# Seven block products for the queries of a cross attention: 14 units of half a block instead of 8 blocks

## What is computed

```python
q = (hn @ w_xq).reshape(Bsz, S, N_XHEADS, DH_X)      # hn = rmsnorm(h) * gain, S = 1024, D = 1024
kv = mn @ w_xkv                                       # mn: 256 normalised memory tokens
s = jnp.einsum('bshd,bmhd->bhsm', q, k) * (DH_X ** -0.5)
p = jax.nn.softmax(s, axis=-1)
o = jnp.einsum('bhsm,bmhd->bshd', p, v).reshape(Bsz, S, D_MODEL)
h = h + o @ w_xo
```

## Time and profile before

| | us |
|---|---|
| median of 3 runs (2746.62 to 2751.62) | 2748.8 |
| profiled execution, its own time | 2748.8 |
| its span in the trace | 2747.0 |
| keys and values (from 386.8 to 438.8) | 52.0 |
| queries, block 41 to the last but one matmul group (from 438.8 to 523.3) | 84.5 |
| TensorE's granted clock, mean | 0.994 of full speed |

### The profile page before, as it was taken

One profiled execution on the slowest core, in us unless ns is written; L12 is line 12 of the kernel. 1 busy time (PEld: TensorE's weight loads), 2 busy tenths in 40 slices (PEclk: granted clock), 3 DMA queues, 4 the chain that ended last, 5 costly groups with the idle time before them and its releaser, 6 DMA issues.

```text
span 2747.0 us, 35390 instructions
## 1 busy us (share of the span) xinstructions
PE 2690.7 (98%) x12702; PEld 2202.3 (80%) x12702; DVE 1782.2 (65%) x2101; ACT 1122.8 (41%) x1862; POOL 1338.7 (49%) x782
## 2 busy tenths in 40 slices
PE   8999999999999999999999999999999999999999
PEld 6888787878778888888887777778887788888886
DVE  7888643345866666976845456884548655557776
ACT  4256623132433333443413525563457333334444
POOL 4323123455689999100466321555165788884002
PEclk9999999999999999999999999999999999999999
DMA  4100324343122222651422110332022443347413
GB/s 155 34 29 31 108 78 152 131 161 115 48 91 72 88 80 80 227 183 32 165 91 95 46 39 24 130 115 92 16 100 92 161 145 125 127 153 268 165 58 138
DMA packets 109866, 291.23 MB, mean 106 GB/s; under 512 B 10032, under 2 KB 20528, under 8 KB 108976
## 3 DMA queue, kind: packets, MB, share of 16 engines
q1 hardware_dynamic: 99488, 256.74, 27.3%
q10 hardware_dynamic: 10256, 32.86, 3.3%
HBM read 230.32 MB, written 59.24 MB: 105 GB/s over the span
## 4 chain that ended last, share of the span: by engine, by line
PE 75%; issue 11%; DVE 6%; POOL 5%; ACT 2%; DMA 1%; ACTq 0%; POOLq 0%; DVEq 0%; SPq 0%
PE products L953 21%; PE others L1448 14%; PE products L1448 12%; PE others L1520 7%; PE products L1520 7%; POOL w_lo L768 2%; PE products L1047 1%; PE others L953 1%; DVE work L2820 1%; POOL w_hi L761 1%; PE products L1076 1%; PE products L1695 1%; DMA w_raw<-wstream 1%; PE products L1359 1%; PE others L1628 1%
## 5 line engine op out<-in xcount | busy, mean ns | idle before, releaser
L953 PE MATMUL products<-act_hi,w_hi 128*128 128x512 f32 x864 | 347.2, 402 | 1.5 <-DVE act_lo L2776 1.3
L761 POOL TENSOR_TENSOR w_hi<-w_raw,small 128x1024 fp32r<-128x1024 f32 x54 | 110.2, 2042 | 480.6 <-PE products L953 297.1
L953 PE MATMUL products<-act_lo,w_hi 128*128 128x512 f32 x864 | 338.0, 391 | 0.0
L953 PE MATMUL products<-act_hi,w_lo 128*128 128x512 f32 x864 | 337.8, 391 | 0.0
L844 POOL TENSOR_TENSOR w_lo<-w_raw,w_hi 128x512 fp32r<-128x512 f32 x200 | 308.7, 1551 | 42.0 <-ACT w_hi L2263 42.0
L953 PEld LDWEIGHTS products<-act_hi,w_hi 128*128 128x128 f32 x864 | 163.3, 189 | 42.3 <-issue 7.3
L2263 ACT ACTIVATE w_hi<-w_raw 128x512 fp32r<-128x512 f32 x240 | 146.2, 626 | 115.8 <-PE products L1448 48.7
L953 PEld LDWEIGHTS products<-act_hi,w_lo 128*128 128x128 f32 x864 | 162.9, 189 | 35.0
L953 PEld LDWEIGHTS products<-act_lo,w_hi 128*128 128x128 f32 x864 | 163.3, 189 | 31.4 <-issue 0.2
L877 POOL TENSOR_TENSOR w_lo<-w_raw,w_hi 128x512 fp32r<-128x512 f32 x8 | 10.3, 1294 | 363.7 <-ACT w_hi L2303 363.7
L768 POOL TENSOR_TENSOR w_lo<-w_raw,w_hi 128x512 fp32r<-128x512 f32 x80 | 126.1, 1597 | 115.8 <-ACT w_hi L2617 115.8
(11 more groups left out here) (626 smaller groups left out, 7338.5 us busy)
## 6 DMA issues: line engine op xcount, KB each, us to landing
w_raw<-wstream SPq DMA_DIRECT2D x155, 512.0 KB, 3.5
w_raw<-wstream SPq DMA_DIRECT2D x168, 256.0 KB, 2.6
work<-wstream SPq DMA_DIRECT2D x52, 512.0 KB, 4.4
parked_sums<-work SPq DMA_DIRECT2D x20, 1024.0 KB, 5.5
parked_hidden<-work SPq DMA_DIRECT2D x40, 512.0 KB, 3.0
raw<-parked_sums SPq DMA_DIRECT2D x28, 512.0 KB, 8.1
raw<-parked_hidden SPq DMA_DIRECT2D x20, 512.0 KB, 6.6
work<-parked_hidden SPq DMA_DIRECT2D x20, 512.0 KB, 7.7
```

The lines of the kernel that those rows point to most:

```text
L761: pool.tensor_tensor(w_hi[:, slot, :], w_raw[:, slot, :], zeros, ALU.add)\
L953: last = pe.matmul(out[:, c], a[:, ws, w], x[:, k, c], start=(k == 0 and i == 0), stop=(k == KT - 1 and i == 2))
```

## The change

The queries are a product of a 2x2 arrangement of weight parts (outputs 0 to 511 and 512 to 1023, inputs 0 to 511 and 512 to 1023) and one of activations (inputs in two halves, tokens in two halves). Eight products of quarters make it in the plain way; the changed kernel makes it of seven, by sums and differences of quarters on both sides.

- The seven products are the `QUERY_STEPS`, each in two units, so `q1` has 14 units of 24 matmuls in place of 8 blocks of 48. A unit's weights are 512 KB, as two pieces of 128x512: from `wstream` for the products first, second and corner (units 0 to 3, 6 and 7), from `query_sums` for the others.
- The weight sums for them are made ahead, by POOL, while ACT and DVE split the keys' and values' blocks: SP loads two blocks at a time into `W[:, 10:14]` (`query_blocks`), POOL makes four sums of each pair, and SP writes 1 MB back (`park_query_sums`), four times in all.
- On the activations, only tokens 0 to 511 are split ahead, in `k1` and `v1`. The sums and differences are made within `q1`: ACT scales quarters, DVE adds and subtracts, ACT makes high parts, DVE low parts, all of 128x512.
- In `q1` from unit 2 on ACT makes `w_hi`, and POOL `w_lo` in two operations of 128x512; before, POOL made both from block 43 on.
- Results come out of PSUM by ACT (`query_copies`) and are added up by DVE (`evacuated`, `last_queries`).
- The root is no longer multiplied into the queries. PE turns it into columns (eight small matmuls, `root_columns`) between units 0 and 1, and the softmax takes it as a scale.
- `move_block(0)` waits for the end of unit 5 and not for the start of `q1`, since `second_lo` lies in its place until then; it stands ahead of unit 7's load. Its sums are made by POOL behind unit 6's split; those of `move_block(1)` and `(2)` behind the splits of units 8 and 10. `cross` and `xo1` keep their work, but for the order of DVE's first steps.

```diff
-STAGES = [("z1", 17, 17), ("out1", 8, 8), ("k1", 8, 8), ("v1", 8, 2), ("q1", 8, 9), ("xo1", 8, 8),
+STAGES = [("z1", 17, 17), ("out1", 8, 8), ("k1", 8, 8), ("v1", 8, 2), ("q1", 14, 17), ("xo1", 8, 8),
...
-                    sp.wait_ge(s("product_quarters"), 4 * BLOCK0["q1"])
+                    sp.wait_ge(s("product_quarters"), 4 * (BLOCK0["q1"] + 6))
...
+            def query_blocks(n):
+
+                if n == 0:
+                    sp.wait_ge(s("product_quarters"), 4 * (BLOCK0["out1"] + 3))
+                elif n == 1:
+                    sp.wait_ge(s("mem_sums"), 1)
+                else:
+                    sp.wait_ge(s("parked_moved"), 16 * (n - 1))
+                for m in range(2):
+                    sp.dma_start(query_sums_at(n)[:, m, :], ap["wstream"][q0 + n + 4 * m]).then_inc(s("block_moved"), 16)
+
+            def park_query_sums(n):
+
                 sp.wait_ge(s("parts_summed"), 4 * n + 4)
...
+                sp.dma_start(query_sums[n].rearrange("m p t -> p m t"), query_sums_at(n)).then_inc(s("parked_moved"), 16)
+
+            def query_unit(u):
+
+                kind, i, slot = QUERY_STEPS[u // 2], u % 2, (q0 + u) % 2
+                m = slice(2 * i, 2 * i + 2)
+                if kind in ("first", "second", "corner"):
+                    m = slice(q0 + 2 * i + 4 * (kind == "corner"), q0 + 2 * i + 4 * (kind == "corner") + 2)
+                    source = ap["wstream"][m, :, half_of(kind != "first")]
+                else:
+                    low, k = {"difference": (0, 0), "last": (0, 1), "lower": (1, 0), "sum": (1, 1)}[kind]
+                    source = query_sums[m, low, :, half_of(k)]
+                    if u == 4:
+                        sp.wait_ge(s("parked_moved"), 64)
+                sp.dma_start(by_half(w_raw[:, slot, :]), source.rearrange("e p t -> p e t")).then_inc(s(f"weights_loaded{slot}"), 16)
...
+            loads(18, 22)
+            for b in range(22, q0 + 3):
+                sp.wait_ge(s("weights_split"), b - 1)
+                if b < q0:
+                    load(b, b % 2)
+                else:
+                    query_unit(b - q0)
+                if b in (22, 23):
+                    query_blocks(b - 22)
+                elif b == 26:
+                    for n in range(2):
+                        park_query_sums(n)
+                        query_blocks(n + 2)
+                elif b in (28, 29):
+                    park_query_sums(b - 26)
...
+                at = b - q0 - MORE
+                if b - q0 == 7:
                     move_block(0)
                 sp.wait_ge(s("weights_split"), b - 1)
-                load(b, b % 2)
-                if at in (4, 6, 8):
-                    park_sums((at - 4) // 2)
-                elif at in (5, 7, 9):
-                    move_block((at - 3) // 2)
-                elif at == 11:
+                if at < KT:
+                    query_unit(b - q0)
+                    if b - q0 in (8, 10, 12):
+                        park_sums((b - q0 - 8) // 2)
+                    elif b - q0 in (9, 11, 13):
+                        move_block((b - q0 - 7) // 2)
+                    continue
+                load(stream_block(b), b % 2)
...
-            relay(BLOCK0["k1"], BLOCK0["q1"] + 2, 0)
...
+            def query_weight_sums(n):
...
+            def weight_sums(n):
...
+            for n in range(4):
+                query_weight_sums(n)
...
-            for b in range(q0 + 2, BLOCK0["ffn1"] + 4):
...
+            for b in range(q0 + 2, BLOCK0["xo1"]):
+                split(b, b // 2, b % 2, lambda b: b + (16 - q0))
+                for n in {6: (0,), 8: (1,), 10: (2,)}.get(b - q0, ()):
+                    weight_sums(n)
...
-                for n in {2: (0,), 4: (1,), 6: (2,), 9: range(3, 8), 10: (8,), 12: (9,)}.get(b - q0, ()):
+                for n in {9: range(3, 8), 10: (8,), 12: (9,)}.get(b - q0 - MORE, ()):
                     weight_sums(n)
...
+                def query_unit(u):
...
+                    if u == 1:
+                        pe.wait_ge(*norm("roots", "q1", 1, 1))
+                    elif kind == "second":
...
+                        pe.wait_ge(*operand_count("operand_lo", "q1", KT))
+                    elif kind == "difference":
+                        pe.wait_ge(s("parts_copied"), 2 * i + 2)
+                        pe.wait_ge(s("factor_lo"), 4)
+                    elif kind == "corner":
+                        pe.wait_ge(s("evacuated"), p + 1 + 2 * i + 2)
+                        pe.wait_ge(s("factor_lo"), 8)
+                    elif kind == "lower":
+                        pe.wait_ge(s("parts_copied"), 4 + 2 * i + 2)
+                        pe.wait_ge(s("factor_lo"), 12)
+                    elif kind == "sum":
+                        pe.wait_ge(s("parts_copied"), 8 + 2 * i + 2)
+                        pe.wait_ge(s("factor_lo"), 20)
+                    elif kind == "last":
+                        pe.wait_ge(s("evacuated"), p + 9 + 2 * i + 2)
+                        pe.wait_ge(s("factor_lo"), 16)
...
+                    last.then_inc(s("product_quarters"), 4)
...
+                def root_columns():
...
+                    pe.wait_ge(*norm("roots", "q1", 1, 1))
+                    pe.wait_ge(s("evacuated"), PROD0["q1"])
+                    for c in range(NCH):
+                        last = pe.matmul(G[:, 0, c:c + 1], rstd[:, c * CH:(c + 1) * CH], ident[:, 0:1], start=True, stop=True)
...
+                def first_queries():
+
+                    query_unit(0)
+                    root_columns()
+                    for u in range(1, 12):
+                        query_unit(u)
                     scores(0)
-                    half_part(b, G[:, p % 2, HALF:T], 1, range(4, 8)).then_inc(s("product_quarters"), 2)
+                    query_unit(12)
                     scores(1)
+                    query_unit(13)
...
+                for k in range(3):
+                    query_scaled(k)
+                query_weight_high(2)
+                query_scaled(3)
+                for k in range(4):
+                    query_factor_high(second_hi[:, k, :], rest_difference[:, k, :], 2 * k + 2)
+                query_copies(lower_of, query_chain, 0, (0, 1), 0)
+                query_weight_high(3)
+                query_copies(lower_of, query_chain, 1, (2, 3), 0)
+                for k in range(4):
+                    query_factor_high(upper(act_hi, k), rest_corner(k), 8 + 2 * k + 2)
+                for k in range(4):
+                    query_factor_high(lower(act_hi, k), rest_lower(k), 8 + 2 * k + 1, 2)
+                query_weight_high(4)
+                for k in range(4):
+                    act.activation(upper(act_hi, 4 + k), upper(W, 4 + k), ACT.Identity, scale=col("x1", 4 + k)).then_inc(s("factor_hi"), 1)
+                query_weight_high(5)
+                for k in range(4):
+                    query_factor_high(lower(act_hi, 4 + k), rest_sum(k), 2 * k + 1, 4)
+                query_weight_high(6)
+                query_copies(upper_of, query_chain, 4, (0, 1), 8)
+                query_weight_high(7)
+                query_copies(upper_of, query_chain, 5, (2, 3), 8)
...
-                if 2 <= n < 5:
+                if 2 <= n < 6:
                     query_high(n - 2)
-                elif KT <= n < KT + 5:
+                elif KT < n < KT + 5:
                     query_high(n - KT + 3)
...
-            for n in range(2):
-                values_high("1", n)
+            first_queries()
...
+                for k in range(4):
+                    dve.wait_ge(s("factor_hi"), 2 * k + 2)
+                    made(dve.tensor_tensor(rest_sum(k), scaled_upper(k), scaled_first(k), ALU.subtract))
+                    dve.wait_ge(s("factor_made"), 2 * k + 1)
+                    made(dve.scalar_tensor_tensor(rest_difference[:, k, :], upper(W, 4 + k), col("x1", 4 + k), rest_sum(k), ALU.mult, ALU.subtract))
+                    if k == 2:
+                        dve.wait_ge(s("token_columns"), 1)
+                        dve.tensor_scalar(small[:, 48:48 + NCH], G[:, 0, 0:NCH], float(D // NH) ** -0.5, None, ALU.mult).then_inc(s("evacuated"), 1)
+                for k in range(4):
+                    low(second_lo[:, k, :], rest_difference[:, k, :], second_hi[:, k, :], 8 + k + 1)
+                for k in range(4):
+                    made(dve.scalar_tensor_tensor(rest_lower(k), upper(W, 4 + k), col("x1", 4 + k), scaled_upper(k), ALU.mult, ALU.subtract))
+                    dve.wait_ge(s("factor_made"), 8 + 2 * k + 1)
+                    made(dve.scalar_tensor_tensor(rest_corner(k), lower(W, 4 + k), col("x1", 4 + k), rest_difference[:, k, :], ALU.mult, ALU.subtract))
+                for k in range(4):
+                    low(upper(act_lo, k), rest_corner(k), upper(act_hi, k), 12 + k + 1)
+                dve.wait_ge(s("parts_copied"), 2)
+                evacuated(2, 0, 10, (0, 1), bank)
+                for k in range(4):
```

(24 more changed lines are left out.)

235 lines of the change are left out of this document (163 added, 72 removed).

## The result

| | before | after |
|---|---|---|
| median of 4 runs each | 2749.0 (2746.6 to 2751.6) | 2781.0 (2779.3 to 2782.0) |
| ratio | | 1.0116 (1.0101 to 1.0131) |
| span of the profiled execution | 2747.0 | 2777.4 |
| first matmul of `k1` to unit 0 (block 41) | 52.0 | 57.4 |
| first matmul of `k1` to the first of the feed forward | 340.2 | 371.8 |

The change costs 32.0 us, where 14.8 were forecast, and the time lies above the range (2778 at the most), and above every rival's number. The direction was right, the size was not. 31.6 us lie between the start of `k1` and the feed forward.

The account below looks back on a forecast made before the run. PE was taken to bound the kernel, with keys and values bound by the feed. From 2748.8: -10.9 + 2.5 + 3.2 + 5.0 + 1.6 + 7.6 + 6.8 - 1.0 = +14.8, so 2763.6 us, range 2750 to 2778.

Parts of the forecast that it names:

- What bounds the kernel: Whole kernel: PE is busy 98% of the span, so time changes only where matmuls go or PE waits.
- matmuls, -10.9: In `q1`: 336 matmuls of 128x512 in place of 384 save 10.9 us.
- Feeding, +2.5: In `k1` and `v1`: block 27's load, late behind query pairs and parks, costs 2.5 us (0 to 5).
- Roots, +3.2: Behind unit 0: PE waits 2.3 us for the roots and spends 0.9 on eight small matmuls; 2.5 to 4 in all.
- Factors, +5.0: Before unit 4: ACT's and DVE's sums, highs and lows delay its weights, so PE waits 5.0 us (1 to 9).
- the rival in which DVE and POOL shut each other out: Before unit 4: each of four POOL operations holds DVE for 1.30 us, 5.2 in place of 1.0; 2767.8 us, 15%.
- The clock, +1.6: Behind unit 4's wait: matmuls at a lowered PE clock lose 1.6 us (0 to 3.2), perhaps again behind unit 11.
- Unit 7, +7.6: Before unit 7: the move held until unit 5's end, its sums and POOL's low parts cost 7.6 us (7 to 9).
- units 9 and 11, +6.8: Before units 9 and 11: a 14.3 us round of park, move and sums against 10.9 of PE, 3.4 us each (6 to 10).
- Chunks, -1.0: Softmax chunks: the first two are done during units 12 and 13, saving 1.0 us (-3 to +1).
- The range: Whole kernel: 2750 to 2778 us, the high end put at about half of the way to all upper bounds, +28.
- The signs: In `q1`: PE's chain breaks before units 4, 7 (longest, 7 to 8 us), 9 and 11 (3 to 4 each).

Follow-up runs that it names:

- experiment 4: Last of the five pairs POOL sums moved one split later in `xo1`: 2776.0 us alone on the changed kernel, 2756.1 on the kernel with sums in halves.
- experiment 7: Changed kernel with block 27's load on SP ahead of the third pair of blocks and the second park: 2781.4 us.
- experiment 6: Changed kernel with unit 1 no longer waiting for the root and the root's columns made behind unit 1: 2780.5 us.
- experiment 8: Kernel with block 27's load forward, POOL's sums of query pairs 2 and 3 cut to 8 columns: 2780.2 us; transfers also cut to 64 columns: 2775.1.
- experiment 2: Changed kernel with ACT's order altered: high parts of units 3 to 6 earlier, factors' high parts for units 8, 10 and 12 behind them: 2772.4 us.
- experiment 5: Changed kernel with useless PE matmuls during two waits, 34 before unit 7 and 16 before unit 11: 2782.5 us.
- experiment 1: Changed kernel with ACT making unit 4's high part behind the first of four corner highs, not behind all eight highs: 2777.3 us.
- experiment 9: Halved sums, later pair, earlier load, root off PE's path, ACT reordered: 2749.5 us; then units 2 and 4 high parts earlier, values' split later: 2747.6; further steps: 2747.8, 2747.1.

## Why the prediction was right and wrong

Two steps failed above all. The five sums that slip against `xo1` had no term of their own, only a place in the +1 at the top of the chunks' bounds; they cost a wait of 3.9 us with half speed behind it, 5.0 us by experiment 4. And the clock, forecast at 1.6 behind one wait, cost 8.7 by the ledger in the queries and `xo1`, and about 2.5 more in `k1`. Against the terms of the forecast the ledger has +2.9 for keys and values, +1.1 for the roots, +1.2 for unit 4, +7.1 for the clock, +1.7 for unit 7, +0.1 for units 9 and 11, -2.0 for the chunks and +3.9 for `xo1`: 16.0 of the 17.2 us by which the forecast fell short.

- **What bounds the kernel** and **matmuls, -10.9**: right. The 336 matmuls are there, and time moved only where PE had to wait.
- **Feeding, +2.5**: 5.4, just outside my 0 to 5, and for another reason. "Only then comes the load of block 27" came true (387.97), but moving it forward gained nothing (experiment 7). I had left DVE out of this term, though I knew the row in which DVE took 2.39 beside POOL, and had priced no clock in this stage.
- **Roots, +3.2**: PE waited 1.49 and the columns took 2.85 (1.8 at full clock), not 0.9; but what was wrong is that this was added at all. It lies beside ACT's and DVE's work for unit 4, and taking it off PE changed the time by 0.5 (experiment 6). It is one chain from the root to unit 4.
- **Factors, +5.0**: 6.17 as a wait. Unit 4's high part started 21.9 behind the root's end (451.23 to 473.14), where I had 17.4. DVE was held four times, as here at L3332, by about 1.0 each, and not 1.0 in all:

```profile
455.99 1.83 DVE L3332 SCALAR_TENSOR_TENSOR tmp<-work,cols 128x512 f32<-128x512 f32 x1
```

```profile
455.99 2.97 POOL L834 TENSOR_TENSOR w_lo<-w_raw,w_hi 128x512 fp32r<-128x512 f32 x2 [56.69 <-ACT w_hi L2511]
474.25 3.37 POOL L834 TENSOR_TENSOR w_lo<-w_raw,w_hi 128x512 fp32r<-128x512 f32 x1 [8.01 <-ACT w_hi L2511]
```

  That is the rival in which DVE and POOL shut each other out (it had 1.3 for each), and it goes both ways: unit 4's first low part on POOL, beside four DVE operations that follow each other from 474.00 to 476.49, took 3.37, where I had 1.3. The operation that was held took 0.9 to 1.1 us more on DVE and 2.1 on POOL. The rule that the Trainium skill states (SBUF — State Buffer, the shared port pair) agrees in kind with these rows and with experiment 8.

  That the wait came out near the forecast is in part luck: unit 4's weights were ready 27.6 after the root, 5.3 later than I had, but PE came 4.2 later too (21.5 and not 17.3), with slow columns and half speed behind them. And the term is not one that the seven products must cost: with another order of ACT's work 4.9 of the 6.2 us are gone (experiment 2).
- **The clock, +1.6**: the term that was furthest off. Half speed came with the columns, behind the waits for units 4, 7 and 11, and behind those in `k1` and `xo1`; the prediction had one, perhaps two of them. "Behind units 7 and 9 it costs nothing" was right for unit 7 (experiment 5). The stretch behind the columns was free too (experiment 6). What is left is 2.5 in `k1`, 1.7 behind unit 4, 1.7 behind unit 11 and 1.5 in `xo1`: 7.4 by the ledger. Unit 11's share is shown by itself in experiment 5 (1.7 to 2.0); the others went away only together with their waits, so their shares are worked out and not shown.
- **Unit 7, +7.6; units 9 and 11, +6.8**: 9.26 and 6.88. The mechanism, the place and nearly the size were right. Unit 7's wait was 1.7 longer: its low parts took 4.4 behind the sums, not 2.6, as DVE split the values beside them. The sums came 16.7 and 15.8 us apart where I had a round of 14.3. That unit 9's wait was not longer but shorter, 2.12 for 3.4, is no merit of the sum: unit 7 had started 1.9 late behind its sums, and PE lost 1.7 at half speed behind it.
- **Chunks, -1.0**: -3.0 for the waits in the chunks, and then 3.9 and 1.5 of half speed in `xo1`. This is the missing term. The prediction names the slip ("start later against the scores") and takes it in at up to +1, with no working. The trace of before gives one: the five sums start 2.0 us behind the third chunk's scores (534.93 and 532.93), and the split of `xo1`'s fourth block is done at 619.7, some 4 ahead of its use. After the change they start 4.6 behind (566.54 and 561.95), the five rounds take 2.5 longer, and the chunks 3.0 less: 4 ahead have become nearly 4 late. By this sum the gain in the chunks was itself a part of the cause.
- **The range**: the sum of all upper bounds is given as +28, with 2778 about half of the way to it. The bounds as they stand add up to -10.9 + 5 + 4 + 9 + 3.2 + 9 + 10 + 1 = +30.3, 2779.1. So 2778 already was nearly all of it, and the measured 2781.0 lies above even that sum. No choice within the bounds would have held it.
- **The signs**: the four waits stand where they were written, unit 7's is the longest, and POOL's low part ends each; units 9 and 11 had 3 to 4 us each and have 2.12 and 4.76. Together they are 22.3 us, twice the matmuls that were saved, so that it is slower was no luck.

## What to carry to other kernels

Between an engine's result and the unit that waits for it, add up the one chain of ACT, DVE and POOL and compare it with PE's work beside it; PE's own waits within that span are not to be added. For helpers on POOL, count each meeting of a POOL and a DVE operation at about 1 us for the one that is held (2.1 where POOL met four of DVE's in a row), and cut the helpers into pieces that fit into the gap of one unit. An algorithm that saves matmuls by many small sums (here 10.9 us) must pay for its traffic and its helpers: with the waits taken out that these experiments found, it came to nothing.

## What the runs showed of the hardware that was not expected

- In the rows of this case PE's clock fell to 1.2 GHz in every one of the waits named above from 3.48 us (experiment 1, unit 5) to 9.26, and in shorter ones it did either: at unit 2 in experiment 6, behind a wait of 2.50, it fell, and at unit 9 of the same run, behind one of 2.46, it stayed. So it is with the columns: 1.49 us of waiting and a fallen clock in the changed kernel, 1.93 and a full one in experiment 2. The stretches in which matmuls run at half speed last 3 to 6 us, in two kernels with the same wait of 3.9 in `xo1` 3.2 (653.46 to 656.61) and 6.1 (626.65 to 632.79).
- The same two loads of a pair took 6.4 us from issue to sums in the changed kernel and 8.3 in experiment 5, whose program is the same there but for PE's useless matmuls, and the waits of a round move with them.
- The first matmul of `k1` lies at 384.6 (experiment 2) and 386.8 (changed kernel), and at 390.0 and 386.5 in the first two kernels of experiment 9, though both of a pair run the same program up to there. A difference of a few us between two single profiles is read from the nearest point that both share.
